# Expert loads of 16 KB runs for experts 4 to 7 in a two-layer trunk with mixtures of experts

## The reference, cut to what matters

```python
def hier_moe(x, w_grp, b_grp, w_rt, b_rt, w_gate, w_up, w_down):
    ...
    gate = (...).reshape(T, N_EXPERTS)      # top-2 of the 4 experts of the best group
    h = jax.nn.silu(jnp.einsum("td,edf->tef", xt, w_gate)) * jnp.einsum("td,edf->tef", xt, w_up)
    y = jnp.einsum("tef,efd->td", h * gate[:, :, None], w_down)
    return y.reshape(B, S, D)
```

## Time and profile before

| what | value |
|---|---|
| median of three runs | 1384.84 us (1384.63 to 1385.26) |
| the profiled execution: span, which is its own time from first to last instruction | 1384.6 us |
| TensorE busy, matmuls | 1344.2 us, 97% |
| VectorE, ScalarE, GpSimd busy | 556.2, 412.7, 42.2 us |
| DMA, data moved | 481.80 MB |
| DMA, share of the 16 engines' span on the queue of SyncE | 85.7% |
| expert loads of 1 MB, in rings, and of 2 MB | 216 and 72 |

### The profile page before, as it was taken

The page is one execution under the profiler, slowest core; times in us unless marked ns, Lnnn a source line. Parts: engine busy times, 40 slices in busy tenths (PEclk is TensorE's granted clock), DMA queues, the critical chain, the costliest instruction groups (busy, mean ns, idle before and its releaser), DMA issues.

```text
span 1384.6 us, 21994 instructions
## 1 busy us (share of the span) xinstructions
PE 1344.2 (97%) x9081; PEld 763.4 (55%) x9081; DVE 556.2 (40%) x906; ACT 412.7 (30%) x636; POOL 42.2 (3%) x35
## 2 busy tenths in 40 slices
PE   9899999999999999999999999999999999999997
PEld 8644444443334458888888877764444444334443
DVE  5813222232222246566665665552322323222223
ACT  5611111111101136665656565531111111111112
POOL 1200000000000000000000000110000000000000
PEclk9999999999999999999999999999999999999999
DMA  9999999999999999644545444579999999999997
GB/s 361 406 421 421 419 421 421 426 427 428 428 428 423 421 394 384 209 157 156 179 141 193 152 152 152 183 263 421 420 421 421 421 426 428 427 428 428 424 420 269
DMA packets 86657, 481.80 MB, mean 348 GB/s; under 512 B 6462, under 2 KB 6672, under 8 KB 47412
## 3 DMA queue, kind: packets, MB, share of 16 engines
q1 hardware_dynamic: 85988, 477.50, 85.7%
q10 hardware_dynamic: 432, 2.65, 0.5%
q0 software_dynamic: 160, 0.52, 0.1%
HBM read 478.56 MB, written 2.10 MB: 347 GB/s over the span
## 4 chain that ended last, share of the span: by engine, by line
issue 53%; PE 34%; DMA 7%; DVE 3%; POOL 1%; ACT 1%; SPq 1%; POOLq 0%; ACTq 0%; DVEq 0%
PE ps L1789 13%; PE ps L1597 7%; DMA ring<-in_moe_w_up 6%; PE ps L1827 5%; PE ps L1678 2%; PE ps L1843 2%; PE ps L1754 1%; PE ps L1755 1%; POOL head_rs L625 1%; DMA bias_row<-in_moe_b_rt 1%; DVE ws L1024 1%; PE ps L1882 1%; PE ps L1816 0%; DVE ps L1354 0%; DVE resid L1357 0%
## 5 line engine op out<-in xcount | busy, mean ns | idle before, releaser
L1789 PE MATMUL ps<-ring,xg 128*64 128x512 f32 x1664 | 388.2, 608 | 19.8 <-DMA ring<-in_moe_w_up 15.4
L1597 PE MATMUL ps<-ws,xs 128*128 128x512 f32 x1632 | 383.8, 393 | 2.6 <-DVE ws L1027 1.1
L1597 PEld LDWEIGHTS ps<-ws,xs 128*128 128x128 f32 x1632 | 304.0, 189 | 70.9 <-DVE ws L1027 3.6
L1789 PEld LDWEIGHTS ps<-ring,xg 128*64 128x64 f32 x1664 | 123.0, 139 | 255.0 <-issue 254.7
L1827 PE MATMUL ps<-ring,hidT 128*64 128x512 f32 x832 | 184.6, 595 | 0.0
L1027 DVE SCALAR_TENSOR_TENSOR ws<-ring,vecs,ws 128x512 fp32r<-128x512 f32 x192 | 134.3, 747 | 87.5 <-ACT ws L646 87.5
L1221 DVE TENSOR_TENSOR y_lo<-ps,y_hi 64x512 fp32r<-64x512 f32 x112 | 77.1, 688 | 191.6 <-ACT y_hi L710 188.9
L646 ACT ACTIVATE ws<-ring,vecs 128x512 fp32r<-128x512 f32 x192 | 127.3, 715 | 83.1 <-PE ps L1597 83.0
L1201 DVE TENSOR_TENSOR resid<-resid,ps 128x512 f32<-128x512 f32 x112 | 72.0, 684 | 170.8 <-PE ps L1755 170.8
L701 ACT ACTIVATE silu_g<-ps,slot_scale 64x512 f32<-64x512 f32 x28 | 19.1, 684 | 402.3 <-PE ps L1789 402.3
L710 ACT ACTIVATE y_hi<-ps 64x512 fp32r<-64x512 f32 x112 | 66.3, 592 | 209.2 <-PE ps L1827 207.2
(11 more groups left out here) (199 smaller groups left out, 825.0 us busy)
## 6 DMA issues: line engine op xcount, KB each, us to landing
ring<-in_moe_w_gate SPq DMA_DIRECT2D x72, 1024.0 KB, 13.9
ring<-in_moe_w_up SPq DMA_DIRECT2D x72, 1024.0 KB, 14.7
ring<-in_moe_w_down SPq DMA_DIRECT2D x72, 1024.0 KB, 15.0
ring<-in_moe_w_gate SPq DMA_DIRECT2D x24, 2048.0 KB, 15.7
ring<-in_moe_w_up SPq DMA_DIRECT2D x24, 2048.0 KB, 20.1
ring<-in_moe_w_down SPq DMA_DIRECT2D x24, 2048.0 KB, 18.5
ring<-in_w_kv SPq DMA_DIRECT2D x32, 1024.0 KB, 5.7
ring<-in_w_q SPq DMA_DIRECT2D x16, 1024.0 KB, 5.4
```

The lines of the kernel that those rows point to most:

```text
L1597: last = mm(ps[:, bank + t, :], xs[:, px, k, cols], ws[:, b, pw, j, :], start=(first and j == 0 and n == 0), stop=(last_unit and j == 1 an ...
L1789: last = mm(ps[CAP * h:CAP * h + CAP, b, :], xg[:, b, k, :], both[h][:, j, :], start=(k == 0), stop=(k == KD - 1))
```

## The change

`WIDE_FROM` becomes `PEELED`, so pairs from 2 on, experts 4 to 13, have the form of 2 MB loads. On SyncE the straight code for expert 4 and the loop for experts 5 to 7 go; the loop of 2 MB loads runs over experts 4 to 13. With it expert 4's loads wait by `free` where they waited by `load`. On TensorE one loop runs over pairs 2 to 5.

```diff
-        WIDE_FROM = 4
+        WIDE_FROM = PEELED
         seconds = [START_MOE[l] + RING_OF[SLOTS * e + m] for l in range(2) for e in range(2 * WIDE_FROM, EXP - 2)
                    for m in range(1, SLOTS, 2)]
...
-                def one_slot(n, e, m):
-
-                    free(e, m)
-                    sp.dma_start(ring_view(n, m), expert_load(l, e, m)).then_inc(slot_loaded[n % SLOTS], 16)
-
-                for m in range(SLOTS):
-                    n = n1 + m
-                    load(n, expert_load(l, 2 * PEELED, m), ring_view(n, m))
-                with sp.Fori(2 * PEELED + 1, 2 * WIDE_FROM) as e:
-                    for m in range(SLOTS):
-                        one_slot(n1 + m, e, m)
                 with sp.Fori(2 * WIDE_FROM, LAST - 1) as e:
                     for m in range(0, SLOTS, 2):
                         free(e, m + 1)
                         two_slots(n1 + m, e, l, m)
...
-                with pe.Fori(PEELED, WIDE_FROM) as i:
-                    pair(i, i - 1, loop=PEELED)
                 with pe.Fori(WIDE_FROM, NPAIR - 2) as i:
                     pair(i, i - 1, loop=WIDE_FROM)
```

## The result

The changed kernel takes 1391.97 us, median of 4 runs (1389.47 to 1394.55); the kernel before, on the same chip, 1384.74 (4 runs). The ratio is 1.0048, 95% interval 1.0035 to 1.0060: slower by about 7 us, where the forecast was 0.8 us less. The profiled execution is the fastest of the four, 1389.47 us with a span of 1387.4, 2.8 longer than the span of before.

A forecast was written before the change was run, and what follows sets the result against it. Transfers were taken to bound the two MoE stages, TensorE being only slightly faster. Layer 0's -0.2 and layer 1's -0.6 us gave -0.8 from a span of 1384.6, 0.2 under the median 1384.84: forecast 1384.0 us, range 1381.6 to 1387.3.

The forecast's parts named there:

- Part 4: Everything else: 48 instead of 96 load instructions, two TensorE loops over pairs made one, less code fetched; costed at nothing.
- What bounds the kernel: In both MoE stages transfers set the end, TensorE being only slightly faster; faster transfers or DMA pauses reach it one for one.
- Part 1: Experts 4 to 7, both layers: 2 MB loads move 48 MB faster than 1 MB loads, gaining 2.0 us per layer (1.6 to 2.6).
- Part 2: Expert 4's first load is issued later, so the queue runs dry; landings slip 1.8 us in layer 0, 1.4 in layer 1.
- Part 3: Coarser buffer release issues the next expert's loads one block later; queue just holds at expert 5, by 0.5 and 0.8 us; no cost.
- rival (b): Queue stays thin at expert 5's loads after expert 4's quarters 2 and 4: +5.2 us, 1390.0, half of it 1387.0; chance 0.12.
- expert 7's third quarter: Tightest point for TensorE: second load lands at 258.2, block begins at 259.1; a wait would only replace part of expert 8's.
- Two signs of being wrong: Listed signs: no dip at about 148 and 1012, a second one at 179 and 189, or load waits changing over 2 us per layer.
- The sum of Parts 1 to 3: Layer 0: -2.0 + 1.8 = -0.2 us; layer 1: -2.0 + 1.4 = -0.6 us; together -0.8, both reaching the end.
- (c): Run length isn't what makes 428 GB/s out of 422, so only the pauses stay: +3.2 us, 1388.0; chance 0.03.
- (a): The pause at expert 4's first load is cheap or covered: 1381.0 or 1382.2; chance 0.22, of which 0.13 below 1382.07.
- (d): Clock: if a layer's last TensorE wait changes sides, the end moves up to 1.7 us either way; no chance of its own.

The follow-up runs named there:

- exact waits: Changed kernel, but expert 4's 2 MB loads wait only for the reads of the buffers they overwrite: 1390.96 us, ratio 1.0048 to the kernel before.
- the kernel with two loops: Changed kernel with all its loads, but TensorE's pairs 2 to 5 in two loops of two pairs: 1388.13 us (1.0018), repeated 1387.08 us (1.0007).
- the kernel with exchanged branches: Changed kernel with layer 0's two branches exchanged, so the usual case falls through and the jump over the overflow code comes before attention: 1393.39 us, 1.0052.

## Why the prediction was wrong

**Part 4 failed**, at "Two loops over pairs become one: at the old entries ... no idle time but the wait for the load; nothing. Less code is fetched; ... at most it is a gain". It looked at the entries of the loops that change, and not at the first jump behind them. What it lacked is the sum that the runs give: 868 instructions less move the target by 100 in its block, to two ahead of the end, and the second block costs 7.61 - 2.06 = 5.5 us on an engine that has no slack there. A row of before pointed at it: the 2.06 us ahead of 398.57 that waited for "issue", not for a load. The prediction took its layer's waits to be five for loads and used this one nowhere. The rule on taken branches, cited above, would have named the place; but it gives no price, and nothing that the prediction had in hand said where the target falls in its block.

**What bounds the kernel** was right up to expert 11 and wrong behind it. "A pause of the DMA engines reaches the end one for one" is not what was seen in layer 0 from 398.57 on: there TensorE doesn't wait for loads, and its own stop, 5.5 us longer, reached the end as 5.2.

**Part 1, the rate, right in kind.** 428 GB/s from 190 to 280; over 155 to 268 it is 426, for the dip at 170 to 190; before, 422 there. That it reaches the end one for one no run shows: where the jump is cured the time is that of the kernel before.

**Part 2, the late load, right in kind.** Forecast: issue at 147.6 and landing at 155.1 by the clock of before, 7.5 after. Measured: issue at 145.94, which is 147.7 with the 1.8 by which this execution was early, landed 7.9 later, at 155.6. In layer 1 issue at 1015.05, with the DMA engines idle for a fifth of 1010 to 1020. Counted from the landing of expert 3's last load, where 4.9 us would be no pause, the landing came after 5.9 us in layer 0 and 6.9 in layer 1, a slip of 1.0 and 2.0 for the forecast 1.8 and 1.4; in other traces of the same loads it is up to 3.0. In the Trainium skill (DMA: Bandwidth & Descriptors, Latency and other measured facts) the first byte comes after some 0.6 us; by that the load would have landed some 1.1 us sooner than the 7.5 of the prediction, and the 7.9 speaks against it again.

**Part 3, costed at nothing, was wrong in that.** It rested on margins of 0.5 and 0.8 us at expert 5's loads. The first of them is issued at 175.09 and lands at 184.9, 5.9 us behind expert 4's last one, where the rate alone gives 4.9; 410 GB/s from 170 to 190 for 428 is a loss of 20 x 18 / 428 = 0.8 us, and layer 1 shows the same at its place (first load of expert 5: 5.9 us behind). That is a weak form of rival (b). From the last landing of expert 3 to the first of expert 8, the kernel before takes 125.3 us in layer 0 and 125.7 in layer 1, the changed one 125.0 and 126.5: -0.2 as forecast in layer 0 and +0.8 for -0.6 in layer 1. One trace doesn't settle tenths: the means over the traces with the old loads (six) and with the new ones (nine, exact waits left out) are 124.9 and 125.4 against 125.9 and 126.2, 1.0 and 0.8 us more in place of the forecast gain. At expert 7's third quarter, named as the tightest point, TensorE did wait:

```profile
258.56 3.65 PE L1778 MATMUL ps<-ring,xg 128*64 128x512 f32 x16 [1.18 <-DMA ring<-in_moe_w_up]
```

**Two signs of being wrong came**, as the prediction named them: the second dip, and waits for loads that changed by over 2 us (7.4 to 9.5 in layer 0, 8.0 to 10.1 in layer 1). In part this is TensorE being faster, not the loads later: from 255 to 285 its granted clock is 1.00 where it was 0.94, and over the span 0.994 where it was 0.990. How much of the change that explains is not known.

**The sum of Parts 1 to 3** was -0.2 in layer 0 and -0.6 in layer 1. On TensorE the table has -0.09 at expert 8, and -0.57 for layer 1, near the forecast; but single traces of one kernel differ by 1 us and more in a layer, so this agreement is in part luck. By the medians, with the jump cured by dead code, it is 1.0002, 1.0000 and 0.9995: no measurable change, as was forecast for everything but the jump. The mechanism behind it is another: the rate's gain was spent on two thin places in the queue and not on one.

**The rivals.** (b) gave 1390.0, near the result, but its mechanism isn't the loss: with the same loads and 8 dead instructions the time is 1384.45. The thin queue that it names is there, at about 1 us. (c) is out, since 428 GB/s came with the longer runs; (a) was not seen. Of (d), the clock shows in the group behind the stop (5.83 us for 16 matmuls, granted 0.50 from 401 to 405; 3.65 at full clock), which is 0.5 more than the 5.35 behind the shorter stop of before.

**Still open.** Why two blocks come 5.6 to 6.4 us apart in every kernel, when a packet itself takes 1.0 us; why the queue loses 1 us at expert 5, where a load was still under way; and the rest of 1 to 3 us that the kernel with two loops keeps.

## What to carry to other kernels

Where code is added or taken out ahead of a jump that is taken, price the jump too: here branch to target took 6 us, less the work already queued, and a target two instructions ahead of the end of a 256-instruction block 5.5 us more. An edit that gains or loses 0.2 to 0.6% for no visible reason is compared with the same edit plus a few instructions that never run, before it is believed. When a wait is removed from a queue, look for the next place where the queue runs thin before the gain is counted. Look for idle time that ends with "issue" behind a branch, and put a jump where another resource has the slack, not where the engine sets the pace.

## What was not expected of the hardware

- A taken jump over the overflow code: 6.0 to 6.5 us from branch to target in all eighteen traces, whatever it jumps to. The jump back in a loop of some 865 instructions: 0.2 to 0.3 us, and no packet on the instruction queue (none from 217.3 to 294.5 in the kernel before, none from 215.9 to 393.3 in the changed one).
- The target's code runs 2.5 to 2.6 us after the start of the packet that brings it (395.76 and 398.36 before; 393.30 and 395.91 after), and the next packet comes 5.6 to 6.4 us after the first, used at once or not.
- Two instructions ahead of a block's end cost 5.5 us, fourteen 4.3 us, and six or more behind it nothing. The effect is in one engine's instruction stream alone: the load queue moved 423 GB/s through the stop (386 to 403).
- Behind the 5.07 us without a matmul in the kernel with exchanged branches, TensorE's granted clock was 0.50 (1.2 GHz) from 519 to 525, and the stage took 7.5 us more, not 5.1.
